# Two transformer blocks in f32 on one core: attentions and scan reordered, dummy matmuls in front, the first norm by row block

## The chip, the core and the metric

The kernel runs on one core of a Trainium2 chip. The metric is the device time of one execution in microseconds (us). Everything is f32 in memory. TensorE is called PE, VectorE DVE, ScalarE ACT, GpSimd POOL, and SyncE SP; they are five engines, each with an instruction stream of its own, which wait for each other by semaphores.

## The reference

256 rows of 1024 channels go through two different blocks of a transformer. Cut to what is computed (`rms` is x / sqrt(mean(x^2) + 1e-6) times a gain):

```python
# block 1
h = rms(x, pre_mix_g)
aq, ak, av, hq, hf_fwd, hf_bwd, hi, hg = split(h @ w_in)      # 512,128,128, 5 x 512
att = softmax attention(rope(rms(aq)), rope(rms(ak)), av)     # 8 heads of 64, 2 for keys
rec = gated scan of (silu(hq), forget gates of hf_fwd / hf_bwd, hi), both directions
rec = rms(rec per head) * silu(hg)
x = x + rms(concat(att, rec) @ w_out, post_mix_g)
h = rms(x, pre_x_g);  m = rms(mem, mem_norm_g)                # 256 rows of memory
x = x + rms(softmax attention(h @ w_xq, m @ w_xkv) @ w_xo, post_x_g)   # 4 heads of 256
h = rms(x, pre_ffn_g)
u = conv over rows, 3 taps, of (h @ w_up)                     # 2 x 2816 columns
x = x + rms((silu(gate) * val) @ w_down, post_ffn_g)
# block 2
z = rms(x, ln_mix_pre) @ w_in2
y_a = rms(softmax(q1 k1) v - lam * softmax(q2 k2) v) @ w_proj_a    # 8 heads, chunk-causal
y_b = latent attention(cq @ w_uq, ckv @ w_ukv) @ w_proj_b          # 8 heads, chunk-causal
x = x + rms((sigmoid(g_a) * y_a + sigmoid(g_b) * y_b) @ w_o)
x = x + rms((silu(h @ w_ffn_gate) * (h @ w_ffn_up)) @ w_ffn_down)
```

## The kernel before, in words

**Rows and tiles.** The 256 rows are two row blocks of 128 partitions (`R` = 2, `r` is 0 or 1). A normalised input is turned into eight tiles of 128 channels x 256 rows (`KT` = 8). The norm of the input does that by matmuls: x's block times a diagonal matrix of the reciprocal roots (`turn_norm`, L682, matmuls L692, the diagonals on DVE L1954). The row's sum of squares is ACT's (L1436), the root is POOL's power (L1289), for both row blocks in one instruction. The memory's norm goes the same way.

**Three products for one.** PE's fast form for f32 rounds its operands, so each operand is split into a high part (a rounding copy) and a low part (the rest), and every product is three matmuls, high x high, high x low, low x high (`products`, L542, matmuls L545). Activations are split on their way out of PSUM (ACT L1451 and DVE L1964, for example).

**The weights' stream.** SP loads chunks of up to 2 MB into a ring of slots. A chunk is used in pieces of 128x1024 elements, in a fixed order for the whole kernel. ACT makes the high part of each piece (L1420), DVE its low part (L1944); those of the chunk xkv2 are POOL's (`split_lo`, L1310). The parts have three places of their own and six lent by other tiles, so a split waits until PE has used the piece that lay there. How far ACT and DVE are ahead of PE is written into their streams by hand: `ahead(upto)` splits all pieces up to a number, `ahead_of(name, n)` up to the n-th piece of a chunk. `reached[...]` holds the number that PE's stream has reached at a named point. Everything queued on an engine behind such a call waits with it.

**Banks of PSUM.** Eight: G[0..3] go round for the results of weights (`next_g`), M[4..7] serve the attentions, norms and FFNs. The class `Banks` (L116) counts who fills and who empties them.

**The order of the work.** First norm; hff, hfb (the forget gates, columns of w_in); the memory's norm; hq. Then the scan as nine levels (`next_level` on DVE, L2108: `double_keys`, keep the level's result with `keep_level`, and so on; `gather_keys` on ACT, L1502), with the remaining chunks of w_in and the first of w_xkv between the levels. Between levels 5 and 8 DVE also does the rope of the first attention's queries and keys (`rope1`), which needs a power of 20 columns on POOL. Then attention 1 in eight units, w_out, the last quarter of w_xkv (xkv3), the norm pre_x, w_xq, the cross attention in four units, w_xo, and the first FFN in 11 iterations. In block 2 follow the products of w_in2, the differential attention, the latent attention ("mla", eight units, with the pieces of w_proj_a between them), w_proj_b, the merge with the two gates, w_o, and the second FFN.

**An attention.** `attend` is there on PE (L794), ACT (L1576) and DVE (L2187). In step n PE makes the scores of unit n (into M[0] or M[1]), turns the probabilities of unit n-1 (L817, into M[2]) and makes the values of unit n-2 (L841 or L892, into M[3]). DVE takes the maximum of the scores (L2215), ACT the exponentials and their sums, one per row block (L1590), and DVE scales them in the *next* step (L2199), before anything else of that step. ACT copies the turned probabilities out, DVE takes the output. Pieces of weights come at the end of steps (`fill`): the eight pieces of xkv1 and xkv2 in steps 0 to 3 of attention 1, nothing in the cross attention, and in "mla" one piece a step. `ahead` calls stand in the middle and at the end of a step on ACT and DVE.

**w_xo and what follows.** w_xo is used by column halves of 512, in pieces of two tiles of channels: a pass over row block 0 (`row_pass`, L606), then over row block 1. The first half of the columns of a row block is complete after four of its eight piece uses. `post_rows_of` (ACT, L1650) squares the result; scaling, residual and the next norm follow on DVE, POOL and ACT, in `into_ffn` (L1669 and L2313), while PE runs row block 1. The FFN's first products of row block 0 come behind.

**The first FFN.** In iteration i, PE does up-pieces for the gate and the value and the down-product of iteration i-1. DVE does the three taps of the convolution (L2394) and splits the down-rows' second piece behind the taps of the gate.

**The merge.** POOL multiplies ACT's sigmoids with the outputs; ACT's order is sigmoids and high parts of w_proj_b's pieces in turns.

## Time and profile before

| | us |
| --- | --- |
| median of 3 runs | 975.42 (974.31 to 978.83) |
| the profiled execution | 976.41 |
| its span | 974.6 |
| PE busy | 917.2 |
| DVE busy | 619.5 |
| ACT busy | 479.6 |
| POOL busy | 87.1 |

The span is the profile's own, from the first to the last record; the execution's time is 1.8 us more. Matmuls with 94% busy time are pipelined, so a busy PE is not PE at its peak. "Granted clock" is the TensorE clock that the throttle gave, as a share of full speed. In the rows below, a bracket `[0.31 <-DVE x L1944]` behind an instruction says that its engine stood idle for 0.31 us before it, and what ended that. The names of tiles are those of the program without their numbers: sb_ring holds raw weights, sb_whi and sb_wlo (or lent2hi, lent2lo and so on) their parts, ps is PSUM.

### The profile page before, as it was taken

The numbers are of one execution on the slowest core, as the hardware profiler recorded it, in microseconds if no ns is written. First come the engines' busy times: TensorE is split into PE (matmuls) and PEld (weight loads), VectorE is DVE, ScalarE is ACT, GpSimd is POOL, SyncE is SP. The second block draws the span as 40 slices with busy tenths as digits, with TensorE's granted clock in tenths as the row PEclk, the third lists the DMA queues.
The fourth block names the chain that finished last, engine by engine and source line by source line (L and its number), as shares of the span: only waits on it lengthen the run. The fifth ranks groups of instructions, "written<-read, shape, count | busy, mean of one in ns | idle before, by whom it ended". The sixth has DMA issues, their size and how long they took to land.

```text
span 974.6 us, 13972 instructions
## 1 busy us (share of the span) xinstructions
PE 917.2 (94%) x5556; PEld 804.0 (82%) x5556; DVE 619.5 (64%) x973; ACT 479.6 (49%) x841; POOL 87.1 (9%) x122
## 2 busy tenths in 40 slices
PE   6999699799989999999999999999898999999997
PEld 5988597479867999989978878788676879999996
DVE  4767774556457857576876666667677684363654
ACT  5844244455436735454553446666445562342541
POOL 1210103000002000000013310002003010000000
PEclk9999799999999999999999999999999999999999
DMA  9434232254335634645543645434225584346451
GB/s 328 175 130 158 82 107 88 85 173 159 123 98 183 217 130 158 217 145 182 207 152 118 217 173 173 135 136 174 87 87 182 163 284 170 130 160 227 135 172 43
DMA packets 92720, 152.56 MB, mean 157 GB/s; under 512 B 1968, under 2 KB 52272, under 8 KB 92400
## 3 DMA queue, kind: packets, MB, share of 16 engines
q1 hardware_dynamic: 92256, 150.94, 45.0%
q8 instruction: 44, 0.72, 0.3%
q10 hardware_dynamic: 288, 0.47, 0.2%
q0 software_dynamic: 112, 0.26, 0.1%
q14 instruction: 20, 0.16, 0.1%
HBM read 150.61 MB, written 1.05 MB: 156 GB/s over the span
## 4 chain that ended last, share of the span: by engine, by line
PE 67%; DVE 13%; ACT 5%; issue 4%; DMA 1%; DVEq 0%; ACTq 0%; POOLq 0%; POOL 0%
PE ps L545 58%; DVE sb_wlo L1944 2%; PE ps L841 2%; ACT sb_whi L1420 2%; DVE sb_b L2394 1%; PE ps L817 1%; DMA sb_ring<-in_w_in 1%; DVE sb_probs L2199 1%; PE ps L642 1%; DVE lent9lo L1944 1%; PE ps L678 1%; DVE lent8lo L1944 1%; PE ps L1060 1%; ACT lent8hi L1420 1%; ACT sb_b L1744 0%
## 5 line engine op out<-in xcount | busy, mean ns | idle before, releaser
L1944 DVE TENSOR_TENSOR sb_wlo<-sb_ring,sb_whi 128x1024 fp32r<-128x1024 f32 (+2 forms) x165 | 196.9, 1212 | 134.6 <-ACT sb_whi L1420 133.9
L1420 ACT ACTIVATE sb_whi<-sb_ring 128x1024 fp32r<-128x1024 f32 (+2 forms) x169 | 172.2, 1041 | 104.6 <-PE ps L545 98.2
L545 PE MATMUL ps<-sb_whi,sb_tbhi 128*128 128x512 f32 (+2 forms) x296 | 116.4, 393 | 3.8 <-DVE sb_wlo L1944 2.3
L545 PE MATMUL ps<-sb_whi,sb_tblo 128*128 128x512 f32 (+2 forms) x296 | 113.4, 383 | 0.0
L545 PE MATMUL ps<-sb_wlo,sb_tbhi 128*128 128x512 f32 (+2 forms) x296 | 113.3, 383 | 0.0
L545 PE MATMUL ps<-sb_whi,sb_tahi 128*128 128x512 f32 (+1 forms) x180 | 70.5, 391 | 9.3 <-DVE sb_wlo L1944 9.0
L545 PEld LDWEIGHTS ps<-sb_whi,sb_tbhi 128*128 128x128 f32 x296 | 55.6, 188 | 16.1 <-DVE sb_wlo L1944 3.6
L545 PE MATMUL ps<-sb_wlo,sb_tahi 128*128 128x512 f32 (+1 forms) x180 | 68.1, 378 | 0.0
L545 PE MATMUL ps<-sb_whi,sb_talo 128*128 128x512 f32 (+1 forms) x180 | 68.1, 378 | 0.0
L545 PEld LDWEIGHTS ps<-sb_whi,sb_tblo 128*128 128x128 f32 x296 | 55.6, 188 | 10.8
L545 PEld LDWEIGHTS ps<-sb_wlo,sb_tbhi 128*128 128x128 f32 x296 | 55.7, 188 | 9.2
L545 PE MATMUL ps<-sb_tahi,sb_whi 128*128 128x256 f32 x216 | 61.8, 286 | 0.6 <-DVE sb_b L2443 0.4
L545 PE MATMUL ps<-sb_talo,sb_whi 128*128 128x256 f32 x216 | 61.1, 283 | 0.0
L545 PE MATMUL ps<-sb_tahi,sb_wlo 128*128 128x256 f32 x216 | 61.1, 283 | 0.0
L545 PE MATMUL ps<-sb_tbhi,sb_whi 128*128 128x256 f32 x208 | 59.8, 287 | 0.0
L1744 ACT ACTIVATE sb_b<-ps,sb_col 128x256 f32<-128x256 f32 x44 | 22.2, 561 | 76.0 <-PE ps L545 76.0
L545 PE MATMUL ps<-sb_tblo,sb_whi 128*128 128x256 f32 x208 | 59.4, 285 | 0.0
L545 PE MATMUL ps<-sb_tbhi,sb_wlo 128*128 128x256 f32 x208 | 59.3, 285 | 0.0
L1903 ACT ACTIVATE sb_b<-ps 128x512 f32<-128x512 f32 x11 | 6.6, 597 | 91.5 <-PE ps L545 91.5
L545 PEld LDWEIGHTS ps<-sb_whi,sb_tahi 128*128 128x128 f32 x180 | 34.4, 191 | 17.8 <-DVE sb_wlo L1944 11.3
L1306 POOL TENSOR_TENSOR sb_st<-sb_st 128x1 f32<-128x1 f32 x14 | 4.1, 292 | 491.4 <-ACT sb_probs L1647 491.4
L1590 ACT ACTIVATE sb_probs<-ps,sb_st 128x256 f32<-128x256 f32 (+1 forms) x40 | 17.8, 449 | 52.8 <-DVE sb_st L2215 29.0
(364 smaller groups left out, 2428.8 us busy)
## 6 DMA issues: line engine op xcount, KB each, us to landing
sb_ring<-in_w_in SPq DMA_DIRECT2D x15, 2048.0 KB, 7.9
sb_ring<-in_w_up SPq DMA_DIRECT2D x22, 1024.0 KB, 5.2
sb_ring<-in_w_down SPq DMA_DIRECT2D x11, 1024.0 KB, 7.2
sb_ring<-in_w_ffn_gate SPq DMA_DIRECT2D x11, 1024.0 KB, 5.3
sb_ring<-in_w_ffn_up SPq DMA_DIRECT2D x11, 1024.0 KB, 5.9
sb_ring<-in_w_ffn_down SPq DMA_DIRECT2D x11, 1024.0 KB, 8.4
sb_ring<-in_w_xkv SPq DMA_DIRECT2D x4, 2048.0 KB, 8.0
sb_ring<-in_w_out SPq DMA_DIRECT2D x2, 2048.0 KB, 7.8
```

The lines of the kernel that those rows point to most:

```text
L545: mm = pe.matmul(o, l[a_], r[b_], start=(start and n == 0), stop=(stop and n == 2), skip_group_check=not check)
L642: mm = pe.transpose(bank[b][:, j * P:(j + 1) * P], src[:, r, k * P:(k + 1) * P], ident)
L678: mm = pe.transpose(bank[b][:, j * S + r * P:j * S + (r + 1) * P], src[:, r, k * P:(k + 1) * P], ident)
L817: mm = pe.transpose(bank[M[2]][:, kt * S + r * P:kt * S + (r + 1) * P], probs[:, u % 4, r * S + kt * P:r * S + (kt + 1) * P], ident)
L841: mm = pe.matmul(o[part:part + w, j * S + q0:(j + 1) * S], v[:, kt, c:c + w], pT[:, kt * S + q0:(kt + 1) * S], start=(kt == 0), stop=(kt = ...
L1060: pe.matmul(bank[M[i]][:, r * S:r * S + n], qaT[d, h, r * P:(r + 1) * P], kaT[d, h, 0:n], start=(r == 0), stop=False, skip_group_check=True)
L1420: act.activation(piece_pair(m)[0], src, ACT.Copy).then_inc(s("hi_done"), 1)
L1590: act.activation(probs[:, u % 4, r * S:r * S + spans[r]], bank[b][:, r * S:r * S + spans[r]], ACT.Exp, bias=smax[name][:, R * u + r:R * u ...
L1744: act.activation(conv[g][:, 2 * j + c, :], bank[banks.at[key][0]][:, c * S:(c + 1) * S], ACT.Identity, bias=COL[:, COL_CONVB + at:COL_CONV ...
L1944: dve.tensor_tensor(low, pieces[m][1], high.bitcast(F32), ALU.subtract).then_inc(s("lo_dve"), 1)
L2199: i = dve.tensor_scalar(p[r], p[r], d[:, r:r + 1], None, ALU.mult)
L2394: dve.scalar_tensor_tensor(dst, src, COL[:, at:at + 1], dst, ALU.mult, ALU.add).then_inc(banks.release(key) if last and c else s("ffn1_tap ...
```

## The change

- **Start.** DVE blanks a tile of probabilities, and PE runs four f32 matmuls of 512 columns on it in front of all work (`WARM`). Squares, roots, diagonals and matmuls of the first norm go by row block. The first weight transfer covers 128 columns of the first chunk, the piece that comes first, instead of half.
- **Memory's norm.** DVE scales the rows, PE turns them (`turn_scaled`).
- **Low parts.** POOL makes none any more; DVE makes those of xkv2 too.
- **Scan.** Keys for the next level are doubled at the end of a level. Before level 6 and 7, ACT and DVE split one piece more (`ahead(reached["level5"] + 2)`), and the rope is cut in two: the turn before a level, the scaling, which needs POOL's power, behind the next.
- **Attentions.** `attend` takes a table of work by step and place ("scored", "turned", "valued"). DVE scales a unit's probabilities in the unit's own step. Each step has one `ahead`, at its end. The pieces in attention 1 are spread over steps 0 to 8, and the turns of the scan's output go between its last steps.
- **xkv3** goes into M[2] and M[3], and ACT takes it inside the next norm.
- **Cross attention.** The second half of w_xq and row block 0 of w_xo come between its steps. For that w_xo is cut by rows: each piece is one tile of channels with all 1024 columns (`xo_piece`, `xo_pass`).
- **into_ffn.** ACT splits the last piece of the chunk before the FFN in front of its first square there, no longer behind it.
- **First FFN.** Both down pieces are split before the gate's taps, on ACT and DVE.
- **Latent attention and merge.** The second turn of the differential attention's output moves to step 2, behind a piece; ACT's sigmoids go behind all splits of w_proj_b.

The diff, cut to its core:

```diff
+            dve.memset(probs[:, 0, :], 0.0).then_inc(s("blank"), 1)
...
-            turn_norm("pre_mix_g", x)
+            pe.wait_ge(s("blank"), 1)
+            for _ in range(WARM):
+                pe.matmul(bank[G[3]][:, :], probs[:, 0, 0:P], probs[:, 0, :], start=True, stop=True)
+            for m in range(4):
+                banks.take(pe, f"pre_mix_g.{m}", M[m], 2)
+            for r in range(R):
+                pe.wait_ge(s("pre_mix_g_diag"), r + 1)
+                for m in range(4):
+                    for j in range(2):
+                        k = 2 * m + j
+                        mm = pe.matmul(bank[M[m]][:, j * S + r * P:j * S + (r + 1) * P],
+                                       x[:, r, k * P:(k + 1) * P], diag[:, r, :], start=True, stop=True)
+                    if r == R - 1:
+                        mm.then_inc(banks.fill(f"pre_mix_g.{m}"), 1)
...
             def next_level(n):
-                if 0 < n < LEVELS:
-                    double_keys(n - 1)
                 ahead(reached[f"level{n}"] + 1)
                 if 0 < n < LEVELS:
                     double_queries(n - 1)
                 keep_level(n)
+                if n < LEVELS - 1:
+                    double_keys(n)
...
-            rope1(0)
+            ahead(reached["level5"] + 2)
+            rope1_turn(0)
             next_level(6)
-            rope1(1)
+            rope1_scale(0)
+            rope1_turn(1)
             next_level(7)
+            rope1_scale(1)
...
             attend("att1", ATT_HEADS, ready1, by_rows(scores1, (S, S)), values1, (S, S),
-                   fill=[(cols_half, ("xkv1", memT, 0)), (cols_half, ("xkv1", memT, 1)),
-                         (gemm_rows, ("xkv2", memT, 0)), (gemm_rows, ("xkv2", memT, 1))])
+                   {(0, "scored"): [(cols_half, "xkv1", memT, 0, (0,))], (1, "scored"): [(cols_half, "xkv1", memT, 0, (1,))],
+                    (2, "valued"): [(cols_half, "xkv1", memT, 1, (0,))], (3, "valued"): [(cols_half, "xkv1", memT, 1, (1,))],
+                    (4, "valued"): [(gemm_rows, "xkv2", memT, (0, 1))], (5, "valued"): [(gemm_rows, "xkv2", memT, (1, 2))],
+                    (6, "valued"): [(turn_rec, 0)],
+                    (7, "valued"): [(gemm_rows, "xkv2", memT, (2, 3))], (8, "scored"): [(gemm_rows, "xkv2", memT, (3, 4))],
+                    (9, "scored"): [(turn_rec, 1)]})
...
             attend("attx", X_HEADS, readyx, by_rows(scoresx, (S, S)), valuesx, (S, S),
+                   {(0, "scored"): [(cols_half, "w_xq1", hTx, 0, (0,))], (1, "scored"): [(cols_half, "w_xq1", hTx, 0, (1,))],
+                    (1, "turned"): [(cols_half, "w_xq1", hTx, 1, (0,))], (2, "turned"): [(cols_half, "w_xq1", hTx, 1, (1,))],
+                    (3, "valued"): [(xo_of, 0)], (4, "valued"): [(xo_of, 1)], (5, "valued"): [(xo_of, 2), (xo_of, 3)]})
...
                 q0, q1 = f"{post}0", f"{post}1"
-                ahead_of(q1, 3)
+                ahead_of(q1, 4)
                 post_rows_of(post, f"{q0}.0", 0, 0)
-                ahead_of(q1, 4)
                 ahead_of(in0, 1)
                 post_rows_of(post, f"{q1}.0", 1, 0)
...
                 for i in range(FF_ITERS):
                     if i >= 2:
-                        ahead_of(f"f{f}.d{i - 1}", 1)
+                        ahead_of(f"f{f}.d{i - 1}", 2)
                     gate(i, i % 2)
                     if i >= 2:
-                        ahead_of(f"f{f}.d{i - 1}", 2)
                         ahead_of(f"f{f}.d{i}", 1) if i == FF_ITERS - 1 else ahead_of(f"f{f}.g{i + 1}", 1)
...
             attend("mla", MLA_HEADS, ready_mla, scores_mla, values_mla, (P, S),
-                   fill=[(ukv_v, (1,)), (run, ((turn_oa, 1), (gemm_rows, *by_piece[0][1])))] + by_piece[1:])
+                   {(0, "valued"): [(ukv_v, 1)]} | {(1 + q, "valued"): [by_piece[q]] for q in range(8)} |
+                   {(2, "valued"): [by_piece[1], (turn_oa, 1)]})
...
-            ahead_of("w_proj_b_20", 4)
+            ahead_of("w_proj_b_21", 4)
-            for r in range(R):
-                for i, gate in enumerate((siga, sigb)):
+            for r in range(R):
+                for gate in (siga, sigb):
                     act.activation(gate[:, r, :], gate[:, r, :], ACT.Sigmoid).then_inc(s("gates"), 1)
-                    if i == 0:
-                        ahead_of("w_proj_b_21", 2 * r + 2)
```

## Rows read from the trace of the kernel before

**Rows 1.** The page, section 1: engine, busy us, share of the span, instructions.

```profile
PE 917.2 (94%) x5556; PEld 804.0 (82%) x5556; DVE 619.5 (64%) x973; ACT 479.6 (49%) x841; POOL 87.1 (9%) x122
```

**Rows 2.** Waits of PE, whole span: waiting line <- releaser: sum, times, longest (us).

```profile
PE ps L817 <- DVE sb_probs L2199: 14.1, 11, 2.2
PE ps L545 <- DVE sb_wlo L1944: 11.6, 9, 7.8
...
PE ps L545 <- DVE sb_b L2252: 1.0, 1, 1.0
```

**Rows 3.** Stretches: window, length, busy of each engine (instructions), granted clock, DMA share, GB/s.

```profile
111.40:121.30 9.90, 5.43 (x14) 4.28 (x15) 7.66 (x13) 3.99 (x5) 0.00 (x0) 0.51 0.41 142
141.70:195.60 53.90, 46.99 (x248) 35.17 (x248) 28.36 (x58) 24.04 (x55) 11.40 (x6) 0.97 0.22 79
152.30:155.50 3.20, 3.20 (x17) 3.20 (x17) 0.84 (x4) 2.94 (x7) 1.06 (x1) 0.54 0.92 314
256.50:281.00 24.50, 18.00 (x79) 14.08 (x80) 9.64 (x22) 10.52 (x25) 0.00 (x0) 0.93 0.04 13
275.20:278.40 3.20, 2.64 (x7) 1.56 (x5) 0.53 (x1) 3.20 (x5) 0.00 (x0) 0.54 0.01 3
677.10:727.70 50.60, 45.43 (x244) 37.59 (x242) 35.52 (x79) 22.27 (x64) 2.02 (x2) 1.00 0.29 100
733.40:741.10 7.70, 5.04 (x20) 3.19 (x19) 7.68 (x5) 6.07 (x7) 6.25 (x3) 1.00 0.65 248
```

**Rows 4.** Timeline, 5 to 20: start, us, instructions, [idle before <- releaser].

```profile
8.12 0.71 POOL L1289 TENSOR_TENSOR sb_st<-sb_st,sb_neghalf 128x2 f32<-128x2 f32 x1
...
8.86 0.48 DVE L1954 TENSOR_SCALAR sb_diag<-sb_col,sb_st 128x128 f32<-128x128 f32 x2 [3.09 <-POOL sb_st L1289]
...
9.40 6.64 PE L692 MATMUL ps<-sb_diag,sb_x 128*128 128x128 f32 x32 [9.40 <-DVE sb_diag L1954]
...
16.95 0.88 DVE L1964 SCALAR_TENSOR_TENSOR sb_talo<-ps,sb_col,sb_tahi 128x256 fp32r<-128x256 f32 x2 [0.28 <-ACT sb_tahi L1451]
```

**Rows 5.** Timeline, 229 to 234, of a later norm.

```profile
229.73 3.73 PE L692 MATMUL ps<-sb_diag,sb_x 128*128 128x128 f32 x32
```

**Rows 6.** Timeline, 99 to 124, in front of level 7.

```profile
105.94 4.04 POOL L1289 TENSOR_TENSOR sb_st<-sb_st,sb_neghalf 128x20 f32<-128x20 f32 x1
...
110.08 0.69 DVE L2149 TENSOR_TENSOR sb_b<-sb_b,sb_st 128x512 f32<-128x512 f32 x1 [2.34 <-POOL sb_st L1289]
...
112.46 1.15 ACT L1513 ACTIVATE sb_b<-sb_b 128x512 f32<-128x512 f32 x2 [12.60 <-issue]
...
114.59 2.36 DVE L1944 TENSOR_TENSOR sb_wlo<-sb_ring,sb_whi 128x1024 fp32r<-128x1024 f32 x2 [2.21 <-ACT sb_whi L1420]
...
115.87 0.79 PE L545 MATMUL ps<-sb_whi,sb_tahi 128*128 128x512 f32 x1 [7.79 <-DVE sb_wlo L1944]
```

**Rows 7.** Groups by form, 141.7 to 195.6: count | busy, mean ns | idle before.

```profile
L1316 POOL TENSOR_TENSOR sb_wlo<-sb_ring,sb_whi 128x1024 fp32r<-128x1024 f32 x4 | 9.6, 2390 | 14.3 <-ACT sb_whi L1420 14.3
...
L1590 ACT ACTIVATE sb_probs<-ps,sb_st 128x256 f32<-128x256 f32 x16 | 7.4, 470 | 20.2 <-DVE sb_st L2215 20.2
L2199 DVE TENSOR_SCALAR sb_probs<-sb_probs,sb_st 128x256 f32<-128x256 f32 x16 | 7.1, 485 | 0.3
...
L2215 DVE TENSOR_REDUCE sb_st<-ps 128x2 f32<-128x512 f32 x8 | 5.5, 687 | 10.0 <-PE ps L853 10.0
```

**Rows 8.** Timeline, 292 to 316, of ACT behind w_xo.

```profile
300.19 0.57 ACT L1647 ACTIVATE sb_probs<-ps 128x512 f32<-128x512 f32 x1
```

**Rows 9.** Timeline, 359 to 366, one iteration of the first FFN.

```profile
362.42 1.65 DVE L2394 SCALAR_TENSOR_TENSOR sb_b<-ps,sb_col,sb_b 128x255 f32<-128x255 f32 x4
...
363.98 1.22 DVE L1944 TENSOR_TENSOR lent9lo<-sb_ring,lent9hi 128x1024 fp32r<-128x1024 f32 x1
...
365.30 0.47 PE L545 MATMUL ps<-lent8hi,sb_tahi 128*128 128x512 f32 x1 [0.31 <-DVE lent9lo L1944]
```

**Rows 10.** Groups by form, 728 to 742, beside the merge.

```profile
L1944 DVE TENSOR_TENSOR lent9lo<-sb_ring,lent9hi 128x1024 fp32r<-128x1024 f32 x1 | 2.3, 2312 | 0.0
```

More of the change, by code:

```diff
@@ L593, in gemm_rows @@
                     if q == 0:
-                        for key in keys:
-                            banks.take(pe, key, next_g(), readers)
+                        for r, key in enumerate(keys):
+                            banks.take(pe, key, into[r] if into else next_g())
                     for r, key in enumerate(keys):
@@ L1324, in _ @@
             rstd_of("mem_norm_g")
-            for m in range(4):
-                pool.wait_ge(*banks.full(f"mem_norm_g.{m}"))
+            pool.wait_ge(s("mem_norm_g_scaled"), R)
             for d, name in enumerate(("ff", "fb")):
@@ L1574, in square_oa, with attend @@
                                    accum_out=stats["oa"][0][:, at:at + 1]).then_inc(s("oa_sq"), 1)
-            def attend(name, units, spans, fill=(), v_every=1, limit=len(pieces)):
-                turned = [u for u in range(units) if (u + 1) % v_every == 0]
+            def attend(name, units, spans, fill):
                 for step in range(units + 1):
@@ L1612, in attend @@
+                            act.activation(probsT[:, u % 2, S + P:2 * S], bank[M[2]][:, S + P:2 * S], ACT.Copy
                                            ).then_inc(banks.release(key), 1)
[L1613 to L1614 removed]
+                    for f, *args in fill.get(step, ()):
                         f(*args)
[L1616 to L1617 removed]
+                    ahead(reached[f"{name}.{step}"] + 2)
@@ L1625, in post @@
+            for r in range(R):
+                take_rows(f"xkv2.{r}", xv[:, r, 0:512])
             def post(name, keys, first=0):
```

301 lines of the change are left out of this document (146 added, 155 removed).

## The prediction

> **What bounds the kernel now.** I read the page's busy shares first: TensorE (PE) is busy 94% of the span [rows 1], so nothing is worth more than what PE stands idle, and what it does at half clock. Of the span of 974.6 us it is not busy in 57.4 us, some 6 of them behind its last matmul. Then I read the waits of PE: the reader is to see that the turns of the softmax in the three attentions wait longest in sum (14.1 us in 11 waits), then one wait of 7.8 us for a low part of a weight piece [rows 2]; the 9.4 us at the start I take from the timeline [rows 4]. Third, stretches with PE's busy time and granted clock [rows 3]: the first attention (141.7 to 195.6) has PE busy for 46.99 of 53.9 us, the cross attention 18.00 of 24.5, the last attention 45.43 of 50.6, the merge behind it 5.04 of 7.7. In two of them, and behind the wait of 7.8 us, the clock is at its lower level, 1.2 GHz (granted 0.51 to 0.54), after PE stood idle for some two microseconds or more. Matmuls that are issued at half clock cost half of their busy time extra: 2.7 us behind the long wait, 1.6 us and 1.3 us in the attentions.
>
> **Part 1, the start: 2.9 us.** Now the 32 matmuls of the first norm begin at 9.40, take 6.64 us, and each of the four banks is complete only at its place in that row [rows 4]. The same form takes 3.73 us at 229.73 [rows 5]: at the start PE runs at half clock, 0.21 against 0.11 us. The change computes the reciprocal root by row block. Block 0's square ends about 1.3 us before block 1's, POOL's power (0.71 us for two columns) follows for one, and one half of the two 0.24 us scalings; so the first half of the matmuls can start at about 7.7, the second at 9.0. The four dummies are 512 columns of f32 where the norm's are 128, so each is four times 2 x 0.21 us = 1.7 us at half clock; behind a memset they fill PE from about 1.2 to between 6.5 and 8. After that PE should be at full clock: block 0 from 7.7 to 9.5, block 1 to 11.3, the first bank complete at 10.0. ScalarE (ACT) has by then split weight piece 0: it waits for a transfer only, and half of the bytes may come sooner or, as rows of 512 bytes, at the same time; I take the same. Then four pairs of tiles at 0.88 us each on VectorE (DVE) [rows 4] from about 11.4 end near 15.0, where now the last begins at 16.95 and ends at 17.8: 2.9 us. If the dummies don't raise the clock the banks are complete 1.7 us later and 1.2 us is left; the upper bound is 3.3. Behind it PE is busy without a gap worth naming until 100, so the shift stays. The memory's norm becomes two scalings of 128x1024 on DVE, some 1.3 us more than the two of 128x128 there; they end about 38, just as PE arrives. The transposes cost what the matmuls did.
>
> **Part 2, the scan: 6 us.** The chain of waits at 100 to 116 reads backwards [rows 6]: PE waits 7.79 us for a low part, that for a high part on ACT, which stood 12.6 us in front of the gathering of keys for level 7; that wanted keys doubled on DVE, which stood behind the rope's last step, which waited 2.34 us for POOL's power of 20 columns (4.04 us from 105.94). The change doubles the keys before the rope, splits the last piece of this weight before gathering, and waits for the power only after level 6. The wait of 7.79 us goes. What is late next is DVE itself: its work up to the second piece of xkv0 is the same but for its two idle stretches, 2.34 and 2.21 us, and for the second rope scaling (1.0 us from 110.08), which moves behind level 7. That is 5.6 us earlier; PE had half a microsecond of slack there. I take 6. PE will stand idle about 2.3 us before level 7, where it waits for level 6 to be kept, and 1.7 us before that second piece. Lower bound 4.5 (only DVE's idle time), upper 10.5 (7.79 and the 2.7 us of half clock, if DVE were no limit).
>
> **Part 3, first attention and scan's output: 6 us.** The eight weight pieces, now all done in steps 0 to 3, are spread over the steps. Idle 6.9 us and 1.6 us of half clock are what can be had [rows 3]. A unit's probabilities now come in its own step: DVE's maximum (0.69 us), two exponentials on ACT (2 x 0.47), two scalings (2 x 0.31 without POOL beside them), with some 0.4 us of handing over: 2.6 us behind the scores. DVE idles about 1.1 us of it, at the head of its line; queued behind are the taking of an older output and one low part (1.22 us), in all 4.8 us a step against PE's 5.3 with a piece in it. So only the ends stay bare: about 1.6 us in step 2 (unit 1's maximum queues behind the scan's last product and a low part), 0.5 us before the last values, 0.3 us for ACT to free two banks. 8.5 less 2.4 is 6. The four low parts that POOL made (2.39 us each) come to DVE; its scalings, which averaged 0.485 us beside POOL, come back to 0.31 [rows 7]. Bounds 4 and 7.5.
>
> **Part 4, xkv3 into banks of its own: 1.0 us**, the wait for L2252 [rows 2]. ACT takes them during the next norm, before that norm's third bank.
>
> **Part 5, cross attention and w_xo by rows: 1 us net.** To be had: 6.5 us idle and 1.3 us half clock, 7.8 [rows 3]; the four w_xq1 pieces and row block 0 of w_xo cover nearly all, I leave 0.3. But the price comes behind. Now a column half of w_xo is complete halfway, and its square and scaling are done early; by K both halves of a row block are complete only at its last piece, T. DVE's look-ahead also puts the low parts of the next two pieces, one behind ACT's second square, in front of its scalings. From T: square and split on ACT to 3.8, low parts to 5.1, scalings and sums to 7.8, squares, POOL's root to 10.0, rows at 10.5; PE wants them at T + 8.2, after six pieces of 1.37 us: 2.3 us idle. Then ACT's square of row block 1's first half (the place of 300.19 in [rows 8]) stands in front of four tiles of the next norm, and now waits for the end of block 1's pass: about 2.6 us in front of the FFN's first piece, with 0.6 more for a late low part behind it. 7.8 - 0.3 - 2.3 - 3.2 = 2.0, less one half-clock stretch of up to 1.6: 1. Bounds -2 and 5 (if the tail is hidden by half).
>
> **Part 6, FFN of block 1: 2.4 us.** In eight iterations PE waits 0.31 us for the second low part of the down rows, which stands behind four taps (1.65 us); the high part is ready two microseconds before [rows 9]. In front of the taps it is done at 363.7, before PE's 365.0. The taps slip 1.2 us, into DVE's idle time. The second FFN has no such gaps.
>
> **Part 7, last attention and merge: 5.4 us.** The attention idles 5.2 us; I leave 2.5 (1.1 before unit 1's probabilities, 0.95 for the bank that DVE empties only after the second half of the first attention output, 0.4 elsewhere): 2.7. The merge idles 2.7 us [rows 3]: POOL's products run beside four low parts, one of which shows 2.31 us against 1.22 [rows 10]. The sigmoids go behind all splits, so the low parts are done by 735.7; POOL starts then, and the first merged half is needed only at 741.4. All 2.7.
>
> **Sum.** 2.9 + 6 + 6 + 1 + 1 + 2.4 + 5.4 = 24.7. The profiled execution took 976.4 us (span 974.6): 951.7. The median of the runs shown is 1.0 us lower, so I say 951. Lower bounds together 13, upper 34: 963 and 942.
>
> **Where the skill bears on it.** In [rows 10] a low part beside POOL's product takes 2312 ns, against 1.22 us elsewhere [rows 9]. The Trainium skill, GPSIMD Engine Reference, section Specifications, says that the engine shares its SBUF interfaces with VectorE and collides with instructions that have two SBUF inputs: by that rule, the trace agrees, and my part 7 is too good, for the same products of POOL now run beside the merge's own sums.
>
> **Rivals.**
> - *The collision moves* (0.10). The two sums of the merge on PE's path, 0.7 us each, last 1.9 times as long as the low parts did: +1.2 us, 952.
> - *New waits drop the clock, and DVE is late in more steps* (0.20). For: each wait of 2 us in [rows 3] was followed by half clock; five new ones at up to 1.6 us give 7, and a late low part every few steps 4 to 5. Against: two such waits of 1.8 us cost nothing. 963.
> - *The dummies don't do what they are for* (0.08): +1.7 us, 953.
> - *w_xo's tail is hidden and the attentions are full* (0.07): 945.
> - *Slower: DVE becomes the bound in the attentions* (0.05). It now waits for its own exponential in each of 20 units. If its step passes PE's, nothing of 9.7 us in the three attentions is won, and each unit adds up to 1.1 us: 961 + 22 = 983. It decides from 0.75 us a unit on, since the other parts are worth 15. Against: 4.8 us against 5.3 a step.
>
> **How the numbers follow.** The forecast case has 0.50, with a range of its own of 946 to 957. With the rivals the range is 943 to 964. Half a per cent, about what a measurement can tell from no change, is 5 us: faster than 970.5 holds all cases but the last and the far end of the second: 0.93; same 0.03; slower 0.04.
>
> **What would show it.** PE's first real matmul near 7.7 and short; no wait above 2.5 us between 100 and 116, but two near level 7; level 8 some 9 us earlier; the first attention in 48 us; two new waits of over 2 us around the norm behind w_xo, with PE's last scores of the cross attention followed by none; no 0.3 us waits in FFN 1; no low part over 1.5 us in the merge. I am wrong if DVE is busy through the attentions with PE waiting in most steps, or if the waits behind w_xo are above 4 us each.

## The result and the profile after

The changed kernel takes 943.41 us (median of 4 runs, 942.00 to 943.75), the kernel before beside it 976.10 us (4 runs, 974.31 to 978.83): a ratio of 0.966, with a 95% interval of 0.9635 to 0.9686. That is 32.7 us faster where 24.4 were forecast (975.4 to 951); the time lies at the lower edge of the stated range of 943 to 964. The profiled execution took 943.75 us, its span is 942.0. Section 1 of its page, to be held against [rows 1]:

```profile
PE 912.0 (97%) x5548; PEld 799.7 (85%) x5548; DVE 620.8 (66%) x978; ACT 479.1 (51%) x841; POOL 80.5 (9%) x120
```

PE is busy 5.2 us less, although the four dummies are in it, and idle 27.4 us less: faster matmuls and fewer waits both count. The waits of PE (columns as in [rows 2]):

```profile
PE ps L542 <- DVE sb_wlo L1978: 5.1, 8, 1.5
PE ps L784 <- DVE sb_b L2107: 3.1, 2, 2.4
PE ps L542 <- DVE sb_tblo L2332: 2.2, 2, 1.6
PE ps L542 <- DVE sb_talo L2013: 2.1, 1, 2.1
PE ps L859 <- DVE sb_probs L2251: 2.0, 2, 1.2
```

L542 are the products (L545 before), L859 the turns of the probabilities (L817 before), L784 the scan. The turns' 14.1 us have become 2.0, and the 7.8 us in front of level 7 are gone; 2.4 and 1.5 us at two places there have come instead. Stretches of the changed kernel: the first attention, three microseconds in it, the cross attention with half of w_xq and row block 0 of w_xo inside it, the last attention, and w_proj_b up to the first turn of the merge (columns as in [rows 3]):

```profile
130.40:181.46 51.06, 47.78 (x250) 35.04 (x249) 31.18 (x61) 24.55 (x57) 1.84 (x2) 0.97 0.23 83
172.00:175.00 3.00, 3.00 (x8) 2.35 (x8) 0.66 (x1) 0.00 (x0) 0.00 (x0) 0.52 0.00 0
230.20:262.57 32.37, 32.37 (x202) 29.61 (x201) 19.01 (x30) 17.40 (x33) 0.00 (x0) 1.00 0.31 108
651.70:698.90 47.20, 44.90 (x244) 37.61 (x242) 35.19 (x79) 22.32 (x64) 2.02 (x2) 1.00 0.30 107
698.90:712.60 13.70, 13.70 (x63) 11.29 (x62) 11.68 (x13) 10.69 (x11) 5.68 (x4) 1.00 0.70 247
```

The cross attention and the merge have no idle time left; the first attention still has 3.3 us, and half clock behind its longest wait.

To see where the 32.6 us of span come from, I took the start of the same matmul in both traces and subtracted. The difference grows stage by stage:

| up to | start before | start after | difference | part won here | forecast |
| --- | --- | --- | --- | --- | --- |
| first product | 15.80 | 12.44 | 3.36 | 3.4 | 2.9 |
| level 0, behind the memory's norm | 55.71 | 50.56 | 5.15 | 1.8 | 0 |
| level 8 of the scan | 134.44 | 123.17 | 11.27 | 6.1 | 6 |
| w_out | 195.65 | 181.46 | 14.19 | 2.9 | 6 |
| norm pre_x | 229.73 | 215.12 | 14.61 | 0.4 | 1 |
| turns for row block 1 in front of the first FFN | 314.47 | 293.85 | 20.62 | 6.0 | 1 |
| behind the first FFN | 498.68 | 473.41 | 25.27 | 4.7 | 2.4 |
| first scores of the last attention | 676.79 | 651.36 | 25.43 | 0.2 | 0 |
| the last attention's last products | 724.27 | 695.48 | 28.79 | 3.4 | 2.7 |
| first turn of the merge, and the end | 745.28 | 712.63 | 32.65 | 3.9 | 2.7 |

One term was too large by 3 us (first attention), four too small: the start with the memory's norm 2.3, the cross attention with w_xo 5, the FFN 2.3, last attention and merge 1.9. The first row of the table holds for this profile of before; how far it carries is said below, at the start.

### The profile page after: what moved, and what is told of

Same layout as the page of the kernel before. It is cut to its first block, busy times and chain, and to the rows that moved or that the text cites. A ratio compares the mean times of both kernels' runs of the same rounds, so it can differ in the third digit from the quotient of the medians.

```text
span 942.0 us, 13962 instructions
## 1 busy us (share of the span) xinstructions
PE 912.0 (97%) x5548; PEld 799.7 (85%) x5548; DVE 620.8 (66%) x978; ACT 479.1 (51%) x841; POOL 80.5 (9%) x120
## 4 chain that ended last, share of the span: by engine, by line
PE 80%; DVE 11%; ACT 4%; issue 3%; DMA 2%; POOL 0%; DVEq 0%; POOLq 0%; ACTq 0%
PE ps L542 70%; DVE sb_wlo L1978 2%; PE ps L881 2%; DMA sb_ring<-in_w_in 2%; ACT sb_whi L1461 1%; PE ps L700 1%; PE ps L664 1%; PE ps L936 1%; PE ps L859 1%; PE ps L726 1%; PE ps L1111 1%; DVE sb_b L2132 1%; ACT sb_probs L1682 0%; DVE sb_b L2107 0%; PE ps L893 0%
## 5 line engine op out<-in xcount | busy, mean ns | idle before, releaser
L1978 DVE TENSOR_TENSOR sb_wlo<-sb_ring,sb_whi 128x1024 fp32r<-128x1024 f32 (+2 forms) x169 | 201.8, 1210 | 106.5 <-ACT sb_whi L1461 105.9
L542 PE MATMUL ps<-sb_whi,sb_tbhi 128*128 128x512 f32 (+2 forms) x296 | 117.2, 396 | 4.9 <-DVE sb_wlo L1978 2.8
L542 PE MATMUL ps<-sb_wlo,sb_tbhi 128*128 128x512 f32 (+2 forms) x296 | 114.2, 386 | 0.0
L542 PE MATMUL ps<-sb_whi,sb_tblo 128*128 128x512 f32 (+2 forms) x296 | 114.1, 385 | 0.0
L542 PEld LDWEIGHTS ps<-sb_whi,sb_tbhi 128*128 128x128 f32 x296 | 56.1, 189 | 17.5 <-DVE sb_wlo L1978 4.6
L542 PE MATMUL ps<-sb_whi,sb_tahi 128*128 128x512 f32 (+1 forms) x180 | 69.5, 386 | 0.7 <-DVE sb_wlo L1978 0.6
L542 PE MATMUL ps<-sb_wlo,sb_tahi 128*128 128x512 f32 (+1 forms) x180 | 67.3, 374 | 0.0
L542 PE MATMUL ps<-sb_whi,sb_talo 128*128 128x512 f32 (+1 forms) x180 | 67.3, 374 | 0.0
L542 PEld LDWEIGHTS ps<-sb_whi,sb_tblo 128*128 128x128 f32 x296 | 56.0, 189 | 10.9
L542 PEld LDWEIGHTS ps<-sb_wlo,sb_tbhi 128*128 128x128 f32 x296 | 56.1, 189 | 9.3
L542 PE MATMUL ps<-sb_tahi,sb_whi 128*128 128x256 f32 x216 | 62.0, 287 | 1.2 <-DVE sb_talo L2002 0.7
L2418 DVE SCALAR_TENSOR_TENSOR sb_b<-ps,sb_col,sb_b 128x255 f32<-128x255 f32 x88 | 36.1, 475 | 40.8 <-ACT sb_b L1782 40.8
L542 PE MATMUL ps<-sb_tbhi,sb_whi 128*128 128x256 f32 x208 | 60.1, 289 | 1.5 <-DVE sb_wlo L1978 1.5
L542 PE MATMUL ps<-sb_talo,sb_whi 128*128 128x256 f32 x216 | 61.1, 283 | 0.0
L542 PE MATMUL ps<-sb_tahi,sb_wlo 128*128 128x256 f32 x216 | 61.1, 283 | 0.0
L542 PE MATMUL ps<-sb_tblo,sb_whi 128*128 128x256 f32 x208 | 58.9, 283 | 0.0
L542 PE MATMUL ps<-sb_tbhi,sb_wlo 128*128 128x256 f32 x208 | 58.9, 283 | 0.0
L542 PEld LDWEIGHTS ps<-sb_tahi,sb_whi 128*128 128x128 f32 x216 | 41.4, 192 | 2.1 <-issue 1.5
```

Of the source, the lines that this page charges most:

```text
L542: mm = pe.matmul(o, l[a_], r[b_], start=(start and n == 0), stop=(stop and n == 2), skip_group_check=not check)
L1978: dve.tensor_tensor(low, pieces[m][1], high.bitcast(F32), ALU.subtract).then_inc(s("lo_done"), 1)
L2418: dve.scalar_tensor_tensor(dst, src, COL[:, at:at + 1], dst, ALU.mult, ALU.add).then_inc(banks.release(key) if last and c else s("ffn1_tap ...
```

## The experiments

Each was timed beside the kernel before, whose median was 975.5 to 977.4 us. Its single times spread from 973.4 to 980.6 us, so sizes below one per cent are read as differences of starts in the traces, as above.

### A wait that stands at the wrong product

The third piece of xkv2 waits 2.07 us in the changed kernel's first attention. The timeline around it:

```profile
169.79 0.69 DVE L2013 TENSOR_TENSOR sb_talo<-ps,sb_tahi 128x512 fp32r<-128x512 f32 x1 [0.16 <-ACT sb_tahi L1499]
...
170.62 0.47 PE L542 MATMUL ps<-sb_whi,sb_tbhi 128*128 128x512 f32 x1 [2.07 <-DVE sb_talo L2013]
```

The product reads sb_tbhi, the memory. What ends its wait is the low part of the scan's turned output (sb_talo), which only w_out reads. In the code `turn_rec` says `operand(4 + 2 * m, ...)`, which files the wait under a tile number, and the next product that touches tile 4 takes it: xkv2's third piece, not w_out.

```diff
             def turn_rec(m):
                 turn(f"recT.{m}", rec, [2 * m, 2 * m + 1], next_g(), 2)
-                operand(4 + 2 * m, f"recT.{m}")
...
             for h in range(ATT_HEADS):
                 operand(h // 2, f"att1.o{h}")
+            for m in range(2):
+                operand(4 + 2 * m, f"recT.{m}")
```

> The changed kernel, with the wait for the turned scan output (recT) registered only for w_out, the product that reads it; in the changed kernel it is registered with a tile number while pieces of xkv2 still follow, and the next product that touches that tile number, xkv2's third piece, takes it. Theory (a misplaced wait): the wait of 2.07 us at 168.56 goes, and with it the half clock behind it (granted 0.52 from 172 to 175, 1.8 us); the first attention becomes 3.5 to 4.3 us shorter, 939.1 to 939.9 us in all. Rival (the piece waits for its own low part, or DVE is simply late there): the wait stays at 2 us and the time at 943.4.

Measured: 939.96 us (939.92 to 940.13). In its timeline the product follows the values without a wait:

```profile
167.33 1.08 PE L881 MATMUL ps<-sb_probsT,sb_b 128*64 128x256 f32 x4
...
168.34 0.50 PE L542 MATMUL ps<-sb_whi,sb_tbhi 128*128 128x512 f32 x1
```

It starts 2.28 us earlier, of which 0.15 were there since the first product, and 24 products later PE is 3.89 us ahead: 1.6 us were half clock. The theory holds; with this wait away the first attention wins 6.7 us, where 6 were forecast.

### The start: dummies, and transposes for diagonals

```diff
-WARM = 4
+WARM = 0
```

> The changed kernel without the four dummy matmuls (WARM = 0). Theory (the dummies only raise the clock for the first norm): the norm's 32 matmul records take 6.6 us again instead of 3.73, half of them before the second row block's diagonal is there, the first product starts 1.5 to 2.5 us later, and since the first products would run at half clock too for a while, the total is 945.0 to 946.5 us. Rival (the gain of 5.15 us up to level 0 is all from the row blocks and the transposes): within 0.5 us of 943.4.

Measured: 945.08 us (944.15 to 946.02). First the changed kernel's timeline of the start, then the one without dummies:

```profile
1.44 6.77 PE L726 MATMUL ps<-sb_probs 128*128 128x512 f32 x8 [1.44 <-DVE sb_probs L2024]
...
8.05 3.73 PE L735 MATMUL ps<-sb_diag,sb_x 128*128 128x128 f32 x32
...
12.44 0.36 PE L542 MATMUL ps<-sb_tahi,sb_whi 128*128 128x256 f32 x1 [0.66 <-DVE sb_talo L2002]
```

```profile
7.72 6.62 PE L735 MATMUL ps<-sb_diag,sb_x 128*128 128x128 f32 x32 [7.72 <-DVE sb_diag L1993]
...
14.33 0.36 PE L542 MATMUL ps<-sb_tahi,sb_whi 128*128 128x256 f32 x1
```

The dummies end 0.3 us late for the norm, and win 1.9 us at the first product; the row blocks and what else changed there are the other 1.5. The theory holds, but for its half clock in the first products: the 1.9 us are 1.9 still at level 0. The start without dummies moves by itself: in the profiles of four kernels whose start is that of before, the first product begins 0.2, 0.9, 1.4 and 1.6 us earlier than in [rows 4], in the last three with a shorter row of norm matmuls (5.2 to 5.7 us). With dummies it begins at 12.1 to 12.4 us in all eight profiles of kernels that have them. The profile of before that the sum was made against had the slowest of these starts, and so had, by its 6.62 us, the one without dummies: 3.4 us for the whole start and 1.9 for the dummies are upper ends, against the other four starts of before the whole is 1.8 to 3.2.

```diff
-            turn_scaled("mem_norm_g")
+            turn_norm("mem_norm_g", mem)
```

(with DVE's scalings of rows replaced by the diagonals, as before.)

> The changed kernel with the memory's norm made as before, by a diagonal matrix (32 matmul records of 128 columns in f32), not by scaled rows and 16 transposes. Theory (a transpose is one pass where an f32 matmul is two): PE needs 1.8 us more there, the shift at level 0 falls from 5.15 to 3.35 us, the total is 945.2 us. Rival (the forecast's: the transposes cost what the matmuls did, and the 1.8 us come from somewhere else): no difference, 943.4 us.

Measured: 944.53 us (943.82 to 945.55); behind the memory's norm PE is 1.8 us later. The two forms stand in the kernel before and in the changed one:

```profile
39.57 3.74 PE L692 MATMUL ps<-sb_diag,sb_b 128*128 128x128 f32 x32
```

```profile
36.25 1.91 PE L700 MATMUL ps<-sb_col,sb_b 128*128 128x128 f32 x16
```

An f32 matmul against a diagonal is recorded twice per tile (32 records for 16 tiles), a transpose once, and in both rows a record starts every 0.11 us. The theory holds, the forecast's "the transposes cost what the matmuls did" is wrong. The span of this profile is that of the changed kernel all the same, because its half clock fell elsewhere (last section).

### The first FFN: what a wait costs

```diff
                 def down_part(i, k, r, c):
+                    if len(held_down[i]) == k:
+                        held_down[i].append(next_piece(f"f{f}.d{i}"))
...
-                    held_down[i] = [next_piece(f"f{f}.d{i}") for _ in range(2)]
+                    held_down[i] = []
```

> The kernel before, with one edit of the FFN part alone: PE waits for the second piece of the down rows where it first uses it, no longer before the first of the pair. ACT's and DVE's orders stay. Theory (a wait between two pipelined matmuls costs its 0.31 us and about 0.23 us more for draining and filling the pipeline again): the eight waits of 0.31 and the one of 0.20 us vanish, since the low part comes 0.31 us late for a piece that PE needs 2.7 us later; the first FFN is 4.3 to 4.7 us shorter, read in the trace, about 971.5 us. Rival A (the forecast's price, the wait as its row shows it): 2.4 us. Rival B (only the order on DVE matters): no gain, and the same waits.

Measured on the kernel before: 970.32 us, ratio 0.9947 (0.9924 to 0.9971), the first FFN 4.5 us shorter. The other edit alone, as it stands on DVE (ACT's order changes in the same way):

```diff
                 for i in range(FF_ITERS):
                     if i >= 2:
-                        ahead_of(f"f{f}.d{i - 1}", 1)
+                        ahead_of(f"f{f}.d{i - 1}", 2)
                     gate(i, i % 2)
-                    if i >= 2:
-                        ahead_of(f"f{f}.d{i - 1}", 2)
```

> The kernel before, with the other edit of the FFN part alone: ACT and DVE split both down pieces in front of the gate's taps. PE's order stays. Theory: the same waits vanish by this edit too, so the two edits are worth 4.3 to 4.7 us each and not together, about 971.5 us. Rival A (the row's price): 2.4 us. Rival B (the taps behind the split are late for ACT's gate, and PE's next down product waits for the product of gate and value): a new wait of up to 1.2 us an iteration, slower by up to 5 us.

Measured: 972.57 us, ratio 0.9965 (0.9945 to 0.9984), the FFN 4.0 us shorter, a little under what was expected. Either edit takes the eight waits of 0.3 us away; the ninth, of 0.20 us, goes with the first edit and grows to 0.57 with the second. Both together (4.7 us) are worth hardly more than one. The forecast priced the waits at 0.31 us each. The kernel before, around one of them, and the changed kernel at the same place:

```profile
364.59 0.28 PE L545 MATMUL ps<-sb_tblo,lent3hi 128*128 128x256 f32 x1
364.71 0.28 PE L545 MATMUL ps<-sb_tbhi,lent3lo 128*128 128x256 f32 x1
365.30 0.47 PE L545 MATMUL ps<-lent8hi,sb_tahi 128*128 128x512 f32 x1 [0.31 <-DVE lent9lo L1944]
365.60 0.39 PE L545 MATMUL ps<-lent8lo,sb_tahi 128*128 128x512 f32 x1
```

```profile
344.07 0.28 PE L542 MATMUL ps<-sb_tbhi,lent3lo 128*128 128x256 f32 x1
344.19 0.40 PE L542 MATMUL ps<-lent8hi,sb_tahi 128*128 128x512 f32 x1
344.42 0.40 PE L542 MATMUL ps<-lent8lo,sb_tahi 128*128 128x512 f32 x1
```

Read the starts, not the gaps. Pipelined matmuls of 256 columns start every 0.12 us though each lasts 0.28. From 364.71 to 365.30 are 0.59 us where 344.07 to 344.19 are 0.12: 0.47 lost, of which the row calls 0.31 idle. The first matmul behind is followed after 0.30 instead of 0.23. Together 0.54 us, and so at each of the eight: such a wait between pipelined matmuls cost 0.23 us more than its row says. Of other waits that edits took away, the extra was 0.27 to 0.28 us each in the merge (below), 0.25 for the 1.59 us behind w_xo, 0.23 and 0.16 for the two in the last attention, 0.07 for the misplaced one of 2.07 us and 0.01 for the 0.46 us behind w_xo. So 0.23 lies in the upper half of what was seen and is no constant.

### The merge

```diff
-            ahead_of("w_proj_b_20", 4)
+            ahead_of("w_proj_b_21", 4)
             for r in range(R):
-                for i, gate in enumerate((siga, sigb)):
+                for gate in (siga, sigb):
                     act.activation(gate[:, r, :], gate[:, r, :], ACT.Sigmoid).then_inc(s("gates"), 1)
-                    if i == 0:
-                        ahead_of("w_proj_b_21", 2 * r + 2)
```

> The kernel before, with the merge part alone: ACT's sigmoids behind all splits of w_proj_b. Theory: POOL's products no longer run beside the low parts, the four waits of 0.93, 0.58, 0.57 and 0.58 us go, each with 0.27 us more for the pipeline, 3.7 to 3.9 us, about 972.2 us; no low part over 1.3 us in the merge. Rival A (the row's price): 2.7 us. Rival B (the collision moves to the merge's sums on PE's path): 1.2 us less than that, and sums that last 1.3 us instead of 0.7.

Measured: 972.00 us, ratio 0.9968 (0.9952 to 0.9985), the merge 3.86 us shorter. Its timeline:

```profile
731.07 1.22 DVE L1942 TENSOR_TENSOR lent2lo<-sb_ring,lent2hi 128x1024 fp32r<-128x1024 f32 x1
732.21 1.22 DVE L1942 TENSOR_TENSOR lent7lo<-sb_ring,lent7hi 128x1024 fp32r<-128x1024 f32 x1
733.48 5.96 POOL L1382 TENSOR_TENSOR sb_b<-sb_b 128x512 f32<-128x512 f32 x4 [56.24 <-ACT sb_b L1878]
...
735.04 1.54 DVE L2591 TENSOR_TENSOR sb_b<-sb_b 128x512 f32<-128x512 f32 x1
...
737.46 0.82 DVE L2591 TENSOR_TENSOR sb_b<-sb_b 128x512 f32<-128x512 f32 x1
```

The low parts are all done before POOL starts, at 1.22 us where [rows 10] had 2.31. The collision did move: the merge's sum beside POOL's products takes 1.54 us and 0.82, where the same sum takes 0.69 without them, but PE's turn comes later, and nothing is lost. The Trainium skill (GPSIMD Engine Reference, Specifications), which the prediction weighed, names DVE instructions with two SBUF inputs among those that contend with POOL. The trace agrees: the sum has two, and the product beside it that reads one input from PSUM stays at 0.69 us. The rule held, and off the path it cost nothing.

### Behind w_xo: who stands in front of the tiles

The changed kernel's timeline in front of the FFN; the product at 268.42 is the first of row block 1:

```profile
267.93 0.60 ACT L1682 ACTIVATE sb_probs<-ps 128x512 f32<-128x512 f32 x1 [6.79 <-PE ps L542]
...
268.42 0.39 PE L542 MATMUL ps<-lent3hi,sb_tahi 128*128 128x512 f32 x1
...
277.39 0.66 PE L664 MATMUL ps<-sb_col,sb_b 128*128 128x128 f32 x4 [0.65 <-DVE sb_b L2323]
...
280.60 0.60 ACT L1682 ACTIVATE sb_probs<-ps 128x512 f32<-128x512 f32 x1 [3.07 <-PE ps L542]
...
281.19 2.17 ACT L1700 ACTIVATE sb_tbhi<-ps,sb_col 128x128 fp32r<-128x128 f32 x8
...
282.85 0.47 PE L542 MATMUL ps<-lent2hi,sb_tbhi 128*128 128x512 f32 x1 [1.59 <-DVE sb_tblo L2332]
```

ACT could have made the tiles from 278.05 on. It waits 3.07 us for the end of w_xo's second pass, for a square that stands in front of them, as the prediction said.

```diff
-                post_rows_of(post, f"{q0}.1", 0, 1)
                 for half in range(2):
                     tiles_hi(norm, T, gain, 0, half)
+                post_rows_of(post, f"{q0}.1", 0, 1)
                 ahead_of(in1, 1)
```

(in the first FFN's call only.)

> The changed kernel with ACT's square of w_xo's first half of row block 1 put behind the high parts of the next norm's tiles of row block 0, in front of which it stands now. Theory: ACT no longer waits there for the end of w_xo's pass (280.60); the wait of 1.59 us in front of the FFN's first product and the 0.46 us behind it go, 2.3 us with the restart of the pipeline, 941.1 us. Rival (the tiles' low parts or POOL's root are next in line at once): under 1 us is won, above 942.4 us.

Measured: 940.46 us (939.65 to 941.41), 2.35 us at the turns for row block 1. The tiles are made at once:

```profile
278.04 1.15 ACT L1700 ACTIVATE sb_tbhi<-ps,sb_col 128x128 fp32r<-128x128 f32 x4 [0.56 <-PE ps L664]
```

### The scan alone

The edits of `next_level`, the rope and the gathering, as the change has them, in the kernel before.

> The kernel before, with the scan's part alone (keys doubled at the end of a level, one split more before the gathering of keys for level 7, the rope in two). Theory (behind the wait of 7.79 us DVE is next in line, as forecast): level 8 comes 5.9 to 6.3 us earlier and the time is about 969.4 us, with new waits of 2.4 us before level 7 and 1.5 us before xkv0's second piece. Rival A (PE gets back its wait and the half clock behind it, 7.8 + 2.7 us): 965 us. Rival B (the new wait of 2.4 us brings half clock of its own): 1.6 us less than the theory, 971 us.

Measured: 968.64 us, ratio 0.9917 (0.9892 to 0.9941). Level 8 comes 6.25 us earlier, of which 0.16 were there before the scan: 6.1 us. The new wait before level 7 is there (2.4 us, the longest of this row); the one of 1.5 us before xkv0's second piece is not. In its place PE runs at half clock behind the first, with DVE busy throughout:

```profile
PE ps L742 <- DVE sb_b L2069: 3.1, 2, 2.4
```

```profile
114.00:116.00 2.00, 2.00 (x12) 2.00 (x12) 2.00 (x6) 0.00 (x0) 0.00 (x0) 0.54 0.28 102
```

So rival B's half clock came, but not its price: DVE was next in line, as the theory has it. In this profile the 6.25 us shrink to 3.9 at the end of the first attention and in the first products of w_out, which have not been touched, and where the granted clock is 0.77 from 180 to 195 (1.00 in the profile of before), and to 2.9 by the end of the cross attention. It is the slowest of the timed runs, and their median does not show that loss: a span can lose elsewhere, by where the clock falls, what a stage has won. The ratio is 8.1 us, 2 more than the scan's 6.1; no trace shows where they come from.

### Low parts on POOL or on DVE

The changed kernel, with `split_lo("xkv2")` on POOL again.

> The changed kernel with the low parts of the four pieces of xkv2 on POOL again. Theory (POOL and DVE slow each other down beside each other, which the step now feels, since a unit's probabilities come in its own step): POOL's low parts last about 2.4 us, DVE's scalings beside them more than 0.4 us instead of 0.31, and PE waits for probabilities or low parts in the steps with xkv2: 944.0 to 946 us. Rival (PE has slack there, and DVE is relieved by four low parts of 1.22 us): 943.4 us or less.

Measured: 943.82 us (942.07 to 943.94), and no matmul moved by more than 0.2 us up to the end. Groups by form, 130.4 to 181.5, with POOL's low parts:

```profile
L1373 POOL TENSOR_TENSOR sb_wlo<-sb_ring,sb_whi 128x1024 fp32r<-128x1024 f32 x4 | 9.5, 2366 | 20.5 <-ACT sb_whi L1476 20.5
...
L2268 DVE TENSOR_SCALAR sb_probs<-sb_probs,sb_st 128x256 f32<-128x256 f32 x16 | 4.9, 351 | 0.3
```

and in the changed kernel:

```profile
L2251 DVE TENSOR_SCALAR sb_probs<-sb_probs,sb_st 128x256 f32<-128x256 f32 x16 | 4.9, 351 | 0.3
```

The time lies between the two forecasts and can't tell them apart; the trace does, and for the rival's mechanism: PE has slack there. The scalings are at 351 ns in both, not the 485 of [rows 7]: it is their new place that keeps them away from POOL, not the move of the low parts. That edit is worth nothing.

### Versions that beat both

The first joins the two mended orders with others: both squares and scalings of w_xo's row block 0 before the next splits, an attention's output taken before the step's other work on DVE, and the second normalisation a step later.

```diff
-                    for f, *args in fill.get(n, ()):
-                        f(*args)
                     if n >= 2:
                         u = n - 2
                         take(u, psum(f"{name}.o{u}")).then_inc(banks.release(f"{name}.o{u}"), 1)
+                    for f, *args in fill.get(n, ()):
+                        f(*args)
...
-                   {0: [(take_v, 1), (normalise_oa, 1)], 2:
+                   {0: [(take_v, 1)], 1: [(normalise_oa, 1)], 2:
```

> A version that should beat both: the changed kernel with recT's wait at w_out, with the tiles before the square behind w_xo, with both squares and scalings of w_xo's row block 0 in front of the next splits (on ACT and DVE), and on DVE with an attention's output taken before the step's other work, and the second normalisation of the differential attention's output one step later. Theory: 3.9 us and 2.3 us as in the single runs, 0.9 us for the wait of 0.65 behind w_xo, 1.4 us and 1.1 us for the waits of 1.24 and 0.96 us in the latent attention, 9.6 us together, 933.8 us (931.5 to 936). Rival (DVE is the bound in the attentions, so what leaves one step is late in the next): the latent attention gains under 1 us and the total stays above 936.5 us.

Measured: 936.07 us (935.96 to 936.35), a shade above the expected range. Won in the trace: 3.7 and 2.3 us as before, 1.4 and 1.2 us in the last attention; lost: 0.35 us behind w_xo, where the splits of the next pieces still stood in front of the scalings (they come with the attention's last `ahead`, not with the line I moved), and 0.9 us at the merge, where w_proj_a's outputs now stand in front of a low part.

```diff
+                if n != 6:
                     ahead(reached[f"level{n}"] + 1)
...
                 keep_level(n)
+                ahead(reached[f"level{n}"] + 1)
...
-                    ahead(reached[f"{name}.{n}"] + 2)
+                    ahead(reached[f"{name}.{n}"] + (0 if (name, n) == ("attx", units + 1) else 2))
```

(and w_proj_a's last outputs behind the attention.)

> The version of before it (936.07 us) with three more orders on DVE: the splits of the next two pieces behind w_xo's scalings, the last outputs of w_proj_a taken behind the splits of the first pieces of w_proj_b, and the level before the last kept in front of one split. Theory: the wait of 0.94 us behind w_xo goes with 0.2 us more, the loss of 0.9 us at the merge goes, and the wait of 2.39 us before level 7 falls to 1.2 us: 3.2 us together, 932.9 us (932 to 934.5). Rival (what is moved behind is late itself, as in the version before): above 935 us.

Measured: 936.30 us (935.52 to 936.75), a miss. Behind w_xo 1.1 us are won, the merge stays. The scan's edit backfires: the wait before level 7 falls from 2.39 to 1.29 us, but the one in front of xkv0's second piece, 1.47 us in the changed kernel, is 2.61, and half clock follows:

```profile
111.00:114.30 3.30, 0.70 (x6) 0.50 (x5) 3.27 (x8) 1.54 (x2) 0.00 (x0) 1.00 0.00 0
114.30:116.00 1.70, 1.69 (x8) 1.69 (x9) 1.70 (x2) 0.00 (x0) 0.00 (x0) 0.54 0.00 0
```

Over the whole stretch this version loses 1.5 us. DVE is busy for 3.27 of 3.30 us there: it is the bound, and another order of its own work only moves the wait.

> The first combined version (936.07 us) with two of the three later orders: the splits of the next two pieces behind w_xo's scalings on DVE (1.1 us in the trace of the version before this one), and w_proj_a's last outputs taken in front of the last unit's output again, as the changed kernel has them (0.9 us back at the merge); the scan as in the changed kernel. Theory: 934.1 us (933.4 to 934.8). Rival (what is won in the attention is lost at the merge again, whatever the order there): 935.0 us or more.

It is the first version with `+ (0 if ...)` and with w_proj_a's last outputs in front again. Measured: 934.10 us (934.02 to 934.26), ratio 0.9562 (0.9536 to 0.9588): 9.3 us below the changed kernel. Section 1 of its page:

```profile
PE 910.7 (98%) x5548; PEld 799.9 (86%) x5548; DVE 621.1 (67%) x978; ACT 479.3 (51%) x841; POOL 79.7 (9%) x120
```

## Why the prediction was right in kind and 8 us short

The step that failed is in part 5, "7.8 - 0.3 - 2.3 - 3.2 = 2.0, less one half-clock stretch of up to 1.6: 1": the cover was sized too small and the price behind it too large, and the stage gave 6.0 us, outside its bounds of -2 and 5, which alone is 5 of the 8. Behind it stand two more mis-sized terms of the same sum, every wait booked at the idle time of its row (the FFN's 2.4 us were 4.7) and "The transposes cost what the matmuls did" (1.8 us put at nothing). The mechanisms of these parts were right; the one of part 3 was not, and it went the other way.

- **Part 1, the start.** Right that the dummies end the slow matmuls: 3.73 us for 32 records, as [rows 5]. The sum went by DVE's last tile, 2.9 us; that tile ends 3.2 us earlier, and the first product starts 3.4 us earlier, against a profile of before with the slowest start. Wrong that the transposes cost what the matmuls did: 1.8 us missed, shown by the kernel with diagonals.
- **Part 2, the scan.** Right, with its mechanism: 6.1 us, waits of 2.39 and 1.47 us where 2.3 and 1.7 were forecast, and nothing back from the half clock beyond what DVE allowed. The change's scan part, put alone into the kernel before, gives the same 6.1 us.
- **Part 3, first attention.** 2.9 us instead of 6. What failed here is "So only the ends stay bare": I read which work stood in which step, but not which instruction takes a registered wait. One line files w_out's wait under a tile number that xkv2 uses first. It cost 2.1 us and, in four of the five profiles that have it, half clock behind it, 1.6 us. Of the ends, the one before the last values held (0.47 us for 0.5), the one at unit 1 was half its size (0.75 for 1.6), and the 0.3 us for ACT's banks did not come. By these the stage should have won more still; against that PE's busy time in it rose from 47.06 to 47.78 us with the same matmuls, and why is open.
- **Part 4.** The wait for L2252 went, one of 0.58 us for a low part came: 0.4 instead of 1.0.
- **Part 5, cross attention and w_xo.** 6.0 instead of 1. The price was 3.2 us, not 5.5; that is what the edits that take its waits away give back, 2.3 us for the tiles and 0.9 for the scalings. The first wait was 0.65 instead of 2.3: ACT's first square begins at 267.93, half a microsecond before row block 0's last piece is through, and the chain of squares, splits, sums and root is ready about 9 us after that piece, not 10.5. The second was 1.59 and 0.46 against 2.6 and 0.6. So the cover won 9.2 us, not 7.5: five waits of 6.4 us by their rows and 1.3 us of half clock were there, and the rest fits some 0.3 us more for each wait. The half clock of up to 1.6 us that I set aside did not come: the clock is 1.00 behind both waits.
- **Part 6, the FFN.** Right place, wrong size: eight waits at 0.54, not 0.31, and a ninth of 0.20 by its row.
- **Part 7.** The last attention won 3.4 (2.7), with the two waits at 1.24 and 0.96 us that were forecast at 1.1 and 0.95; the merge 3.9 (2.7), its four waits at 0.27 us more each.
- **The rivals.** The collision moved, and was off the path. The dummies did what they were for. DVE is not the bound of the first attention: the kernel that gives its four low parts to POOL is no faster. For the other two no run tests it; PE's idle time there is gone or down to 2.3 us. "w_xo's tail is hidden" (945) came nearest, for another reason.
- **The signs.** Level 8 came 11.3 us earlier (9 announced), the first attention took 51 us (48), and the two waits behind w_xo, announced at over 2 us, were 0.65 and 1.59.

Taken together: PE had 47 waits of 0.2 us or more and has 28. I booked each at its row; 19 times 0.23 us would be 4.4 us of the 8, an estimate from the FFN's waits, and a high one, as the other extras were 0.01 to 0.28. The transposes are 1.8, w_xo's price 2.3 and its missing half clock up to 1.6; the first attention's 3 us go the other way. The range's lower end was built from the same rows, so it was too high by the waits' share; besides, the parts' upper bounds (where a part has none, its value) add up to 35 us, not 34, and 34 off the profiled 976.4 is 942, not 943.

## What to carry to other kernels

Price a wait between pipelined matmuls by the starts on both sides of it, not by the idle time in the row; the FFN's waits of 0.31 us were worth 0.54. Where a program files waits under a name and lets the next user take them, follow each moved line to the instruction that will carry the wait. An engine that is idle in front of work that is ready, as ACT was 3.07 us behind w_xo, has something at the head of its queue that the next need does not want: move that, but not where the engine is busy throughout, as DVE in the scan.

## What the runs showed of the hardware

The granted clock does not follow from the length of one wait. A wait of 2.07 us was followed by 0.52 in the changed kernel (172 to 175, the second row of the stretches above). The same wait, of the same length, in the kernel with diagonals:

```profile
172.18 0.47 PE L542 MATMUL ps<-sb_whi,sb_tbhi 128*128 128x512 f32 x1 [2.07 <-DVE sb_talo L2011]
```

```profile
172.00:175.00 3.00, 2.82 (x12) 2.36 (x13) 2.11 (x4) 0.25 (x1) 0.00 (x0) 1.00 0.00 0
```

stayed at 1.00. There the half clock had come sixty microseconds earlier, behind the wait of 2.4 us in front of level 7, which the changed kernel passes at 1.00. First that kernel, then the changed one:

```profile
109.00:113.00 4.00, 3.37 (x17) 3.40 (x18) 4.00 (x10) 0.00 (x0) 0.48 (x1) 0.57 0.56 209
```

```profile
109.00:113.00 4.00, 3.97 (x34) 3.76 (x33) 3.96 (x11) 0.00 (x0) 0.00 (x0) 1.00 0.17 60
```

Behind such a wait the level can stay at the upper (2.4 GHz) or fall to the lower (1.2 GHz); what decides it these runs don't settle. What it costs depends on the place. In the first attention 1.6 us are gone. In the scan DVE is the bound, a slower PE only uses up the 1.47 us that it would wait in front of xkv0's second piece, and nothing is lost. The first and the last of the combined versions have half clock there too (0.70 and 0.58 from 109 to 113), and lose nothing by it: up to level 8 they stand to the changed kernel as they did before the scan. At the start the records say 1.00 throughout, while the same 32 records take 6.62 us without and 3.73 us with dummies ahead of them: there the level has to be read from the length of the matmuls, 0.21 us a record against 0.11.
